# PEER experts of a hybrid decoder step: gelu kept in PSUM, the second table's remainder on VectorE in two pieces

## The reference

```
    def block(args):
        xb, ib, gb = args
        hid = jnp.einsum('td,thkd->thk', xb, u_tab[ib]).astype(F32)
        hid = jax.nn.gelu(hid, approximate=False) * gb
        return jnp.einsum('thk,thkd->td', hid.astype(xb.dtype), v_tab[ib])
```

## Time and profile before

| what | us |
|---|---|
| median of 3 runs | 3093.1 (3090.99 to 3093.38) |
| the profiled execution | 3090.84 |
| its span, first to last instruction | 3089.7 |
| VectorE busy | 2033.2 (66%) |
| TensorE busy, matmuls | 2410.4 (78%) |
| GpSimd busy | 1095.0 (35%) |
| expert loop, first gelu of pair 1 to that of pair 63 | 1655.78 to 3053.63 |

### The profile page before, as it was taken

The page is one execution under the profiler, slowest core; times in us unless marked ns, Lnnn a source line. Parts: engine busy times, 40 slices in busy tenths (PEclk is TensorE's granted clock), DMA queues, the critical chain, the costliest instruction groups (busy, mean ns, idle before and its releaser), DMA issues. The chain is left out here.

```text
span 3089.7 us, 49756 instructions
## 1 busy us (share of the span) xinstructions
PE 2410.4 (78%) x17079; PEld 2159.8 (70%) x17079; DVE 2033.2 (66%) x3749; ACT 775.1 (25%) x1389; POOL 1095.0 (35%) x1131
## 2 busy tenths in 40 slices
PE   4965885586969679604847999899988889889898
PEld 3964774244349678503637889888888888888887
DVE  3137554756731417998956776777778787787877
ACT  1111000122212211004953222222222222222221
POOL 2410000001313311326944545445454544545443
PEclk8976887665979889856978999999999999999999
DMA  2310000123812212100587556556555555555552
GB/s 65 88 36 1 3 3 21 41 83 101 271 46 72 70 55 62 34 0 0 138 194 285 205 201 214 204 201 211 199 199 211 206 198 200 201 207 205 199 199 94
DMA packets 207541, 403.48 MB, mean 131 GB/s; under 512 B 12798, under 2 KB 134073, under 8 KB 190810
## 3 DMA queue, kind: packets, MB, share of 16 engines
q1 hardware_dynamic: 165210, 251.21, 25.0%
q0 software_dynamic: 42240, 151.03, 14.6%
HBM read 370.81 MB, written 31.39 MB: 130 GB/s over the span
## 5 line engine op out<-in xcount | busy, mean ns | idle before, releaser
L2029 DVE TENSOR_TENSOR experts_G<-experts_G,experts_M 128x392 f32<-128x392 f32 x128 | 369.5, 2887 | 330.3 <-ACT experts_G L1928 330.2
L1883 PE MATMUL experts_pV<-experts_GH,experts_VH 128*128 128x392 f32 x1024 | 404.7, 395 | 27.9 <-DVE keep_xT L2033 27.2
L1883 PE MATMUL experts_pV<-experts_GL,experts_VH 128*128 128x392 f32 x1024 | 369.8, 361 | 0.0
L1883 PE MATMUL experts_pV<-experts_GH,experts_VL 128*128 128x392 f32 x1024 | 369.0, 360 | 0.0
L1872 PE MATMUL experts_pH<-keep_xh,experts_UH 128*128 128x392 f32 x1024 | 351.3, 343 | 0.0
L1872 PE MATMUL experts_pH<-keep_xl,experts_UH 128*128 128x392 f32 x1024 | 349.3, 341 | 0.0
L1872 PE MATMUL experts_pH<-keep_xh,experts_UL 128*128 128x392 f32 x1024 | 348.4, 340 | 0.0
L1975 POOL TENSOR_TENSOR experts_VL<-experts_V,experts_VH 128x2048 fp32r<-128x2048 f32 x64 | 295.3, 4614 | 19.3 <-ACT experts_VH L1922 18.0
L2033 DVE TENSOR_TENSOR keep_xT<-experts_pV,keep_xT 128x392 f32<-128x392 f32 x512 | 282.3, 552 | 1.6 <-PE experts_pV L1883 1.5
L1862 PE MATMUL experts_pU<-keep_ident,experts_U 128*128 128x128 f32 x1024 | 167.6, 290 | 117.2 <-DVE experts_UL L2023 109.0
L1883 PEld LDWEIGHTS experts_pV<-experts_GH,experts_VH 128*128 128x128 f32 x1024 | 208.2, 203 | 56.8 <-DVE keep_xT L2033 54.1
(11 more groups left out here) (424 smaller groups left out, 5164.3 us busy)
## 6 DMA issues: line engine op xcount, KB each, us to landing
experts_U<-in_peer_u SPq DMA_DIRECT2D x64, 1024.0 KB, 4.8
experts_V<-in_peer_v SPq DMA_DIRECT2D x64, 1024.0 KB, 5.2
experts_M<-scratch_gates SPq DMA_DIRECT2D x64, 392.0 KB, 3.2
keep_K<-in_cache_k SPq DMA_DIRECT2D x64, 256.0 KB, 3.1
keep_V<-in_cache_v POOLq DMA_DIRECT2D x64, 256.0 KB, 3.7
scratch_gates<-spread_M SPq DMA_DIRECT2D x2, 8192.0 KB, 33.0
inp_w<-in_w_in SPq DMA_DIRECT2D x22, 512.0 KB, 3.8
scratch_gates<-spread_M SPq DMA_DIRECT2D x1, 8704.0 KB, 35.6
```

Source lines behind the costliest of these rows:

```text
L1883: last = nc.tensor.matmul(pV[n % 4][:, 0:ND], l, r, start=(t == 0), stop=(t == 5))
L2029: nc.vector.tensor_tensor(G[e][:, :], G[e][:, :], M[q.b][:, e, :], ALU.mult).then_inc(gated, 1)
```

## The change

Three things are changed. ScalarE's gelu writes its result back to the PSUM bank that it read. VectorE's gating reads it from there, and writes G in SBUF as before; it takes over gelu's wait for the previous pair's G remainder, and TensorE waits for the gating and no longer for gelu before it fills the bank again. The V remainder leaves GpSimd: VectorE computes it in two pieces of 1024 columns, in the loop both between gating 0 and gating 1, in the first and the last pair one before each gating. Waits on `v_lo` count two for each pair.

```
-            sc(nc)(G[e][:, :], pH[e][:, 0:ND], ACT.Gelu).then_inc(gelued, 1)
+            sc(nc)(pH[e][:, 0:ND], pH[e][:, 0:ND], ACT.Gelu).then_inc(gelued, 1)
...
-        def rest_v(pool, q):
-            pool.wait_ge(v_hi, q.count(1, 1))
-            nc.gpsimd.tensor_tensor(VL[q.b][:, :, :], V[q.b][:, :, :], VH[q.b][:, :, :].bitcast(F32), ALU.subtract).then_inc(v_lo, 1)
+        def rest_v(dve, q, e):
+            dve.wait_ge(v_hi, q.count(1, 1))
+            nc.vector.tensor_tensor(VL[q.b][:, e, :], V[q.b][:, e, :], VH[q.b][:, e, :].bitcast(F32), ALU.subtract).then_inc(v_lo, 1)
...
             dve.wait_ge(gelued, q.count(2, e + 1))
-            nc.vector.tensor_tensor(G[e][:, :], G[e][:, :], M[q.b][:, e, :], ALU.mult).then_inc(gated, 1)
+            if q.after(1):
+                dve.wait_ge(g_lo, q.count(2, e - 1))
+            nc.vector.tensor_tensor(G[e][:, :], pH[e][:, 0:ND], M[q.b][:, e, :], ALU.mult).then_inc(gated, 1)
...
-                for e in range(2):
-                    gate(dve, q, e)
+                gate(dve, q, 0)
+                rest_v(dve, q, 0)
+                rest_v(dve, q, 1)
+                gate(dve, q, 1)
```

More of the change, by code:

```diff
@@ L1846, in load @@
             if q.after(2):
-                sp.wait_ge(v_lo, q.count(1, -1))
+                sp.wait_ge(v_lo, q.count(2, -2))
             sp.dma_start(V[k][:, :, :], vv[:, at2, :]).then_inc(v_in[k], 16)
@@ L1868, in product_u @@
                 if q.after(1):
-                    pe.wait_ge(gelued, q.count(2, e - 1))
+                    pe.wait_ge(gated, q.count(2, e - 1))
                 for k in range(KD):
@@ L1877, in product_v @@
             if n == 0:
-                pe.wait_ge(v_lo, q.count(1, 1))
+                pe.wait_ge(v_lo, q.count(2, 2))
                 pe.wait_ge(g_lo, q.count(2, 2))
@@ L1925, in gelu @@
             act.wait_ge(hidden, q.count(2, e + 1))
-            if q.after(1):
-                act.wait_ge(g_lo, q.count(2, e - 1))
-            sc(nc)(G[e][:, :], pH[e][:, 0:ND], ACT.Gelu).then_inc(gelued, 1)
+            sc(nc)(pH[e][:, 0:ND], pH[e][:, 0:ND], ACT.Gelu).then_inc(gelued, 1)
         def cut_g(act, q, e):
@@ L1991, in halves_of @@
             def halves_of(q):
-                rest_v(pool, q)
                 rest_g(pool, q, 0)
@@ L2063, in first @@
                 for e in range(2):
+                    rest_v(dve, Pair(0), e)
                     gate(dve, Pair(0), e)
@@ L2092, in tail @@
                 for e in range(2):
+                    rest_v(dve, Pair(NQ - 1), e)
                     gate(dve, Pair(NQ - 1), e)
```

## The result

| | before | after |
|---|---|---|
| median of 4 runs each, us | 3092.05 (3088.96 to 3093.38) | 2859.97 (2856.64 to 2861.93) |
| profiled execution, us | 3090.84 | 2856.64 |
| its span, us | 3089.7 | 2855.6 |
| VectorE busy, us | 2033.2 | 1903.2 |
| GpSimd busy, us | 1095.0 | 834.2 |

What follows compares the result with a forecast made beforehand. Bound: a chain of VectorE's dots, GpSimd's fetches and 4.6 us V subtraction, gating, UL subtraction, then TensorE. Freed, 62 steps fall from 22.55 to 18.9 us, -226.0 from 3090.84, forecast 2865 us; range 2852 to 2950.

Steps and rivals of the forecast that it cites:

- the port rival: Loop: VectorE's pieces held by GpSimd instead of its gating; 2896 us, or 2982 as a ring; chance 0.21.
- The pace of TensorE: Loop step without waits: 8.6 us of hidden product plus four blocks of 2.58, 18.9 us instead of 22.55.
- The gating from PSUM: VectorE's gating, reading gelu's result from PSUM, takes 0.55 us and is never held; the second took 5.99 or 2.66.
- The pieces: VectorE's two V subtractions per pair, 1024 columns each: 1.21 us each, 2.4 per pair, priced like an undisturbed dot.
- The bound of 2.3 us: Upper bound for each V piece on VectorE, from GpSimd's own rate, 4.6 / 2.
- The cover: Between the gatings: the pieces cost nothing, because VectorE's wait for gelu 1 covers them, from 2.3 to 4.7 us.
- the rival with the held pieces: The port case: pieces of 2.3 us each give 2896 us; waiting for four fetches and one remainder, 2982; chance 0.21.
- Gating 1's end: In a loop step, behind gelu 0: 5.4 us, or 5.9 to 6.3 if one G remainder gets between the pieces.
- gelu to PSUM: ScalarE's gelu writing PSUM in place keeps its 0.50 us; even twice that would be covered.
- the clock rival: Loop: a half-speed spell of 2.5 us still comes every second step without any wait; 77 us lost, 2942; chance 0.07.
- The slower rival: Loop: pieces at GpSimd's rate that also wait behind every fetch; 23.0 us a step, 3119 us; chance 0.04.
- The sum: Whole kernel: 62 steps x 18.9 = 1171.8 instead of 1397.85, -226.0; first and last pair unchanged; 3090.84 becomes 2864.8.

Runs made afterwards that it cites:

- the reordered kernel: The changed kernel with both V remainder pieces behind gating 1 instead of between gating 0 and gating 1; 2945.1 us, ratio 0.9517.

## Why the prediction was right

*The bound before.* In the loop of the kernel before TensorE stood idle for 104.4 us until UL subtractions ended and for 26.8 until adds ended, by the waits view. The chain of fetches, V remainder, gating and UL subtraction is what the kernel with one fetch and the one with the move alone both show. Not seen in it was that the hold would pass to the next VectorE instruction if only the gating were freed; the port rival spoke of the pieces alone.

*The pace of TensorE.* Forecast 18.9 us from 8.6 and 4 x 2.58, measured 18.89, blocks 2.58 apart. This term carries the whole forecast: 226.0 forecast, 226.9 measured.

*The gating from PSUM.* 0.55 forecast, 0.563 on average, never held. The mechanism was right, but I did not ask what it is worth by itself. It is worth nothing in the loop once the V remainder is gone, and 28 us (0.9%) without the move, 24 of them in the loop.

*The pieces.* 1.21 forecast; 1.22 where undisturbed, 1.41 on average with the holds. The weighted adds of the second half, which the working took as no longer than the dots from two averages that hold waits, are a little longer undisturbed, 1.27 against 1.21; VectorE had the room. The bound of 2.3 us was not needed: the dot was the right neighbour. The cover is real and its price is known from the reordered kernel: 85 us, 81 of them in the loop. By the trace the rival with the held pieces got the mechanism right and the size wrong: one G remainder gets in (3.21 instead of 2.36), never four fetches. In the other pattern the piece goes first and the fetch is held.

The rule of the Trainium skill that I had weighed (SBUF — State Buffer, "SBUF: two separate sides") gives the port to whoever starts first, for the whole instruction; for a VectorE instruction with two SBUF inputs the page says so only against a GpSimd instruction that reads SBUF. The G remainder and the pieces agree (3.21 us in the second pattern). Whether a row fetch is such an instruction no run here shows; that it is held is measured, 1.69 us instead of 0.94.

*Gating 1's end.* 5.4, or 5.9 to 6.3 when held; measured 5.5 and 6.0.

*gelu to PSUM.* 0.50 kept, 0.482 measured, and gelu 1 stays 4.30 us behind gelu 0 in the loop. In the first and the last pair it is 4.51 behind, against 4.6 forecast.

*The clock.* 1.00 throughout the loop, as forecast; the clock rival has fallen. The working priced a half-speed spell at 2.5 us, from two steps' lengths; the 0.86 of the 24.9 us step says 0.14 x 24.9 = 3.5. Over the loop of the kernel before the mean was 0.946: the 1.2 GHz level was granted for 150 us, and for 10 of these TensorE was idle. By my estimate, then, up to (150 - 10) / 2 = 70 of the 227 us won in the loop are the clock's. It is part of what the waits cost and not a second cause: each of the 34 spells stood beside an idle time of TensorE of over 1 us.

*The slower rival.* It needed pieces of over 4.15 us together that also wait behind every fetch; the longest hold of a piece is one G remainder.

*The sum.* 2864.8 was the forecast for the profiled execution, which took 2856.6. Of the 8.2 us between, 0.9 are the loop and 0.7 the part behind it. 3.3 are the first pair, a term of the sum that I had left at zero: its gating 1 took 2.46 us beside the V remainder there too, and now takes 0.57. The working named that gain in half a sentence and then did not count it. The last 3.3 are the scatter ahead of the first gelu. The median of the runs lies 3.3 above the profiled execution, which leaves 5; that these last two cancel is luck.

## What to carry to other kernels

When VectorE and GpSimd block each other, freeing one victim passes the hold to the next VectorE instruction with its data in SBUF, however small; take the long GpSimd instruction away, or put it where VectorE idles. Work moved to a busier engine is free if it fits in a wait of that engine which something else ends: find that wait in the brackets of the timeline, add the pieces to its start, and see what the first instruction behind it may cost. And divide a step by its bound engine's own rows where it does not wait: that figure, 18.9 us, was here within 0.1% of the 18.89 measured.

## What the runs showed of the hardware that I had not expected

- A VectorE copy of 128x4 floats from SBUF to SBUF took 6.26 us beside GpSimd's subtractions, 0.15 to 0.17 when alone. What spares an instruction the hold is an operand in PSUM (gating 0.57 beside the same subtraction), not a small size.
- Two GpSimd instructions queued behind each other with their inputs ready are one block for VectorE: 4.74 us for both pieces and 1.00 for the next, gating 6.56. In the reordered kernel it is otherwise: there ScalarE's copy for the second G remainder ends only about when the first remainder does, 0.65 us behind the handing over of the first piece, and in 60 of 64 pairs the waiting piece goes ahead of it (the 3.02 us for the two G remainders are 1.04 and 1.90). Two VectorE pieces queued behind each other are no block for GpSimd: a G remainder gets in between them in 29 of 62 steps of the changed kernel.
- A GpSimd row fetch is held by VectorE's subtraction as well: 1.69 and 1.85 us instead of 0.94. If a piece is half of its 2.36 us pair, the first ends at 1992.76 and at 2208.41, and both fetches end 0.86 us later, while the second piece runs undisturbed. So a fetch seems to need the port at its start alone. All fetches of the changed kernel from the first pair on say the same: 36 began beside a piece and took 0.94 to 1.96 us; 59 in whose course a piece began took at most 0.99.
- The other way round: a gating with two SBUF inputs took 0.57 beside a fetch, and so did all 54 gatings of the kernel before that were handed over during one of the first three fetches of a pair. But the weighted add of 3.78 us and the gating of 6.56 us were handed over during a fetch too and did not get through. In both of these it was the last of the four, with a GpSimd subtraction directly behind it (0.02 us). That alone is not the reason. Over all the profiled kernels, second pieces left aside, 68 VectorE instructions were held in this way; each was handed over 0.29 us or more behind the start of the last fetch, and the input of the GpSimd subtraction behind it had been ready for 2.4 us or more. Not held were 18 that were handed over at most 0.25 us behind that start, and 31 first pieces whose G remainder got its input from ScalarE only 0.4 us later. So it looks as if GpSimd keeps the port for its next instruction where that has its input in good time, and not where it comes late, as in the reordered kernel. No experiment was made for it.
- The granted clock stayed at 1.00 over the whole loop in the five kernels in which TensorE was never idle for longer than 0.83 us at a time (the reordered kernel, 0.25 and 0.28 in its rows, has 35.6 us of idle time in 1180). It lies at 0.86 in the long step of the kernel before, behind 2.14 us of idle time. Of the 52 idle times of over 1 us in that loop 34 had a spell at the 1.2 GHz level at their end or just behind it, the other 18 had none; in the kernel without the UL term 1 of 30 had one, the longest, 2.13 us.
